# Expert lists loaded on GpSimd's queue, expert 1's rows gathered whole, and weights stored slab by slab

## The reference, cut to what matters

```python
cap = EC_FACTOR * (B * T) // N_EXPERTS          # 128 latent tokens per expert (16 of the context)
aff = jax.nn.softmax((xt @ router_w).astype(jnp.float32), axis=-1)
gate_vals, idx = lax.top_k(aff.T, cap)
xe = xt[idx]
hid = jax.nn.silu(jnp.einsum('ecd,edf->ecf', xe, w1)) * jnp.einsum('ecd,edf->ecf', xe, w3)
ye = jnp.einsum('ecf,efd->ecd', hid, w2) * gate_vals[..., None]
y = jnp.zeros_like(xt).at[idx.reshape(-1)].add(ye.reshape(-1, D))
```

## Time and profile before

| | |
|---|---|
| Median of 3 runs | 1631.14 us (1629.53 to 1637.18) |
| The profiled execution | 1631.1 us, of which the span from first to last instruction is 1629.3 us |
| PE busy | 1580.3 us (97%) |
| DVE, ACT, POOL busy | 716.6, 387.4, 477.5 us |
| DMA traffic | 324.85 MB |
| Expert part | from 849.7 us; PE then passes an expert in some 47 us |

### The profile page before, as it was taken

One profiled execution on the slowest core, in us unless ns is written; L12 is line 12 of the kernel. 1 busy time (PEld: TensorE's weight loads), 2 busy tenths in 40 slices (PEclk: granted clock), 3 DMA queues, 4 the chain that ended last, 5 costly groups with the idle time before them and its releaser, 6 DMA issues. The chain is left out here.

```text
span 1629.3 us, 28403 instructions
## 1 busy us (share of the span) xinstructions
PE 1580.3 (97%) x11180; PEld 1377.1 (85%) x11180; DVE 716.6 (44%) x1871; ACT 387.4 (24%) x970; POOL 477.5 (29%) x560
## 2 busy tenths in 40 slices
PE   6999999999999899999988999999999999999997
PEld 5866876666668767788878999999999999999997
DVE  4001046776565844222364244444334454433344
ACT  5210113341221466411131111111111111111114
POOL 3000000015232643121203343433344343334432
PEclk9999999999999999999999999999999999999999
DMA  9302212132202486423269899999899999999985
GB/s 346 114 11 85 82 39 59 36 125 30 59 29 93 133 239 204 157 66 103 91 212 353 290 299 297 316 322 298 278 293 304 291 315 329 299 286 285 315 263 228
DMA packets 225582, 324.85 MB, mean 199 GB/s; under 512 B 36015, under 2 KB 116008, under 8 KB 225466
## 3 DMA queue, kind: packets, MB, share of 16 engines
q1 hardware_dynamic: 185817, 282.70, 51.7%
q0 software_dynamic: 15568, 17.45, 5.7%
q10 hardware_dynamic: 24080, 23.02, 4.8%
HBM read 294.42 MB, written 25.51 MB: 196 GB/s over the span
## 5 line engine op out<-in xcount | busy, mean ns | idle before, releaser
L1973 PE MATMUL psum<-arena 128*128 128x144 f32 x4096 | 504.5, 286 | 1.7 <-DVE arena L2615 1.7
L1973 PEld LDWEIGHTS psum<-arena 128*128 128x128 f32 x4096 | 502.8, 190 | 1.9 <-ACT arena L1350 1.9
L1985 PE MATMUL psum<-arena 128*128 128x144 f32 x2048 | 257.3, 288 | 6.3 <-ACT arena L1391 5.0
L1985 PEld LDWEIGHTS psum<-arena 128*128 128x128 f32 x2048 | 254.8, 192 | 7.1 <-ACT arena L1391 5.2
L1556 PE MATMUL psum<-arena 128*128 128x384 f32 x720 | 242.9, 493 | 0.0
L889 POOL DMA_INDIRECT expert_list<-gt x128 | 129.8, 1014 | 317.2 <-DVE gt L2645 287.6
L1556 PEld LDWEIGHTS psum<-arena 128*128 128x128 f32 x720 | 134.5, 191 | 90.0 <-issue 2.9
L2675 DVE TENSOR_TENSOR arena<-gt,psum 128x144 f32<-128x144 f32 x128 | 38.8, 303 | 360.8 <-PE psum L1973 359.8
L2497 DVE SCALAR_TENSOR_TENSOR arena<-arena,gt 128x1024 f32<-128x1024 f32 x128 | 159.1, 1280 | 0.5 <-DMA arena<-affinity_rows 0.5
L1559 PE MATMUL psum<-arena 128*128 128x256 f32 (+2 forms) x784 | 146.4, 346 | 0.0
L1559 PEld LDWEIGHTS psum<-arena 128*128 128x128 f32 x784 | 129.4, 190 | 15.5 <-issue 1.7
(11 more groups left out here) (379 smaller groups left out, 1629.4 us busy)
## 6 DMA issues: line engine op xcount, KB each, us to landing
arena<-in_exp_w SPq DMA_DIRECT2D x96, 2048.0 KB, 11.8
arena<-in_ada_w SPq DMA_DIRECT2D x24, 1024.0 KB, 7.0
arena<-in_w_in SPq DMA_DIRECT2D x11, 1024.0 KB, 5.2
arena<-in_x_sample SPq DMA_DIRECT2D x16, 512.0 KB, 4.8
arena<-affinity_rows SPq DMA_DIRECT2D x16, 512.0 KB
arena<-m_decay_rows ACTq DMA_DIRECT2D x36, 128.0 KB, 3.2
arena<-decay_rows ACTq DMA_DIRECT2D x24, 192.0 KB, 3.4
out<-arena SPq DMA_DIRECT2D x9, 512.0 KB, 2.6
```

The lines of the kernel that those rows point to most:

```text
L1973: ins = mm(bank[:, 0:SLOTS], w[:, k, col], xeT[:, k, :], start=(k == 0), stop=(k == KD - 1))
L1985: ins = mm(bk[4 + db % 2][:, 0:SLOTS], wslot[4 + db // 4][:, k, (db % 4) * P:(db % 4) * P + P], hid[:, k, :], start=(k == 0), stop=(k == K ...
```

## The change

1. **Lists.** `load_list` leaves SP. POOL issues the list loads itself: list 1 right after it is scattered, as plain rows in one DMA; the same list again as four quarter loads inside `expert_rows(0)`; every list e + 2, in four quarter loads, right behind `expert_rows(e)`; list 15 as one DMA of rows. `expert_rows(e + 1)` begins with the wait for that list.
2. **Expert 1's rows** are gathered whole by one indirect DMA in `expert_rows(0, x_rows=True)`, and PE turns them between `hidden(0)` and `second(0)`, as it does for the last expert.
3. **Layout.** The host writes `ada_w`, `w_in`, `w_out` and the three expert matrices to DRAM slab by slab, partition by partition, so that a partition's part of a load is one run of 8 KB (slabs) or 16 KB (expert parts). SBUF holds what it held. The host's work is not in the time.

```diff
-                sp.dma_start(ring[:, s % RING, :, 0:n], w_src[mat][:, :, a:a + n]).then_inc(slab_in[s % RING], 16)
+                sp.dma_start(ring[:, s % RING, :, 0:n], slab_source(s)).then_inc(slab_in[s % RING], 16)
...
             def expert_slab(e, q):
-                one = one.rearrange("e p k f -> (e p) k f")
-                sp.dma_start(wslot[q], one[:, :, 512 * half_q:512 * half_q + 512]).then_inc(w_in_slot[q], 16)
+                src = (exp_w1, exp_w3)[q % 2][e, q // 2] if q < 4 else exp_w2[e, q - 4]
+                sp.dma_start(wslot[q], src.rearrange("p (k f) -> p k f", k=KD)).then_inc(w_in_slot[q], 16)
...
                 if e + 1 < NE:
-                    load_list(e + 1)
                     load_row(e + 2)
...
             scatter_list(1)
+            def load_list(e, rows=False):
+                pool.wait_ge(list_sc, 16 * NL * e)
+                pool.sem_inc(idx_set, 1)
+                if rows:
+                    o = 2 if e == 1 else 8 * e
+                    pool.dma_start(lists[:, o:o + 2], list_d[0:P, :]).then_inc(list_in, 16)
+                else:
+                    load_quarters(e)
+            def load_quarters(e):
+                for c in range(4):
+                    dst = lists[32 * c:32 * c + 32, bass.ds(e * 8, 8)].rearrange("p (a w) -> p a w", w=2)
+                    pool.dma_start(dst, list_d[0:P, :].rearrange("(a i) w -> i a w", i=32)).then_inc(list_in, 16)
+            load_list(1, rows=True)
...
             def expert_rows(e, x_rows=False, y_rows=False):
-                pool.wait_ge(list_in, listed(e + 1))
+                pool.wait_ge(list_in, 16 if isinstance(e, int) and e == 0 else listed(e + 1))
...
+                if isinstance(e, int) and e == 0:
+                    load_quarters(1)
+                    pool.wait_ge(list_in, listed(1))
                 scatter_list(e + 2)
...
-            expert_rows(0, y_rows=True)
-            with pool.Fori(1, NE - 2) as e:
+            expert_rows(0, x_rows=True, y_rows=True)
+            load_list(2)
+            with pool.Fori(1, NE - 3) as e:
                 expert_rows(e)
+                load_list(e + 2)
+            expert_rows(NE - 3)
+            load_list(NE - 1, rows=True)
             expert_rows(NE - 2, x_rows=True)
...
                 hidden(e)
-                if e == NE - 2:
-                    pe.wait_ge(xgl_in, fetched(NE - 1))
+                if e in (0, NE - 2):
+                    pe.wait_ge(xgl_in, fetched(e + 1))
                     pe.wait_ge(e_yeA, e + 1)
                     pe.wait_ge(e_yeD, e + 1)
                     x_turn_latent(0, KD)
...
+    def column_slabs(w, n):
+        return w.reshape(KD, P, -1, n).transpose(2, 1, 0, 3).reshape(-1, P, KD * n)
```

More of the change, by code:

```diff
@@ L66, in plan_slabs, with slab_starts @@
             + win1[4:] + win2 + [None, None] + ada[8:] + wout)
+def slab_starts(slabs):
+    starts, used = {}, 0
+    for s, slab in enumerate(slabs):
+        if slab is not None and slab[0] == "win":
+            starts[s] = used
+            used += D * slab[2]
+    return starts
 def plan_groups():
@@ L171, in hybrid_layer, with slab_source @@
     A_S = [0, 1, 3, 4, 5, 7, 8, 9]
[L172 to L175, removed]
+    in_first = slab_starts(slabs)
+    def slab_source(s):
+        mat, a, n = slabs[s]
+        if mat == "win":
+            return w_in[in_first[s]:in_first[s] + D * n].rearrange("(p k n) -> p k n", p=P, n=n)
+        return {"ada": ada_w, "wout": w_out}[mat][a // SLAB].rearrange("p (k n) -> p k n", n=n)
     def dram(name, shape):
@@ L477, in listed @@
         def listed(e):
-            return 64 * e + 1 if not isinstance(e, int) or e < NE - 1 else 64 * (NE - 2) + 17
+            return 64 * e + 16 if not isinstance(e, int) or e < NE - 1 else 64 * (NE - 2) + 32
         def fetched(e):
-            return 64 * e + 16 if not isinstance(e, int) or e < NE - 1 else 64 * (NE - 2) + 32
+            return 64 * e - 32 if not isinstance(e, int) or e < NE - 1 else 64 * (NE - 3) + 48
         def added(e):
@@ L534, in load_slab @@
                     return
-                mat, a, n = slabs[s]
+                n = slabs[s][2]
                 read = [t for t in range(s % RING, s, RING) if t in last_read]
@@ L655, in load_row @@
                                             ap=[[0, P], [1, NL * P]])).then_inc(row_in, 16)
[L657 to L665, removed]
             sp.wait_ge(r_act, 5)
@@ L674, in _ @@
                 expert_slab(0, q)
-            load_list(1)
             load_row(2)
@@ L906, in expert_rows @@
             def expert_rows(e, x_rows=False, y_rows=False):
-                pool.wait_ge(list_in, listed(e + 1))
+                pool.wait_ge(list_in, 16 if isinstance(e, int) and e == 0 else listed(e + 1))
                 pool.wait_ge(ex_full, e + 1)
-                pool.wait_ge(xgl_in, fetched(e))
+                pool.wait_ge(xgl_in, 16 if isinstance(e, int) and e == 0 else fetched(e))
                 if x_rows:
-                    pool.tensor_copy(icur[:, 0:1], lists[:, 8 * e + 8:8 * e + 9]).then_inc(idx_set, 3)
-                else:
-                    quarter_ids(icur[:, 0:4], e + 1, e * 10 + 5)
-                pool.wait_ge(idx_set, e * 10 + 5)
+                    o = 2 if e == 0 else 8 * e + 8
+                    pool.tensor_copy(icur[:, 0:1], lists[:, o:o + 1]).then_inc(idx_set, 3)
+                else:
+                    quarter_ids(icur[:, 0:4], e + 1, e * 11 + 6)
+                pool.wait_ge(idx_set, e * 11 + 6)
                 pool.sem_inc(idx_set, 1)
@@ L927, in expert_rows @@
                 else:
-                    quarter_ids(icur[:, 4:8], e, e * 10 + 11)
-                pool.wait_ge(idx_set, e * 10 + 11)
+                    quarter_ids(icur[:, 4:8], e, e * 11 + 12)
+                pool.wait_ge(idx_set, e * 11 + 12)
                 pool.wait_ge(e_yeA, e + 2)
@@ L2624, in _ @@
             dve.sem_inc(e_yeD, 1)
-            dve.sem_inc(list_in, 1)
             dve.wait_ge(acc_init, 16 * NL)
             def rank_begin(e):
-                dve.wait_ge(list_in, listed(e - 1))
+                if not isinstance(e, int) or e > 1:
+                    dve.wait_ge(list_in, listed(e - 1))
                 v.tensor_copy(acur, aff[:, 1:NT, bass.ds(e, 1)].rearrange("p a b -> p (a b)")).then_inc(rank_step, 1)
@@ L2676, in expert @@
                         .then_inc(e_hid, 1)
-                    if fb == KD - 2 and not (is_first or is_last or x_rows):
+                    if fb == KD - 2 and not (is_last or x_rows):
                         x_turned(e + 1)
-                if is_first:
-                    x_turned(e + 1)
                 if is_last:
@@ L2719, in expert @@
                 ins.then_inc(e_yeD, 1)
-            expert(0, True)
+            expert(0, True, x_rows=True)
             with dve.Fori(1, NE - 2) as e:
@@ L2759 @@
     rpb[192:-192] = rows
+    def column_slabs(w, n):
+        return w.reshape(KD, P, -1, n).transpose(2, 1, 0, 3).reshape(-1, P, KD * n)
+    w_tiles = _np.concatenate([column_slabs(w_cols[:, a:a + n], n).reshape(-1)
+                               for m, a, n in (x for x in plan_slabs() if x is not None) if m == "win"])
     order = _np.arange(D).reshape(P, KD).T.reshape(-1)
```

12 lines of the change are left out of this document (4 added, 8 removed).

## The result

The changed kernel takes 1817.75 us (median of 4 runs, 1812.44 to 1822.27) against 1632.29 us for the kernel before beside it: 1.1131 times as long, 95% interval 1.109 to 1.1173. The prediction was 1727, its range 1640 to 1790. The direction was right and the size was not; the time lies 28 us above the range. Every ratio here is of fast runs alone; one of the four runs with the layout alone (1686.17 us) was slow and is not in its ratio.

What follows compares the result with a forecast made beforehand. The prediction took PE, busy 97% of the span, as the bound, with POOL's chain only 1.4 us of slack from becoming it. 1631.1 - 1.5 - 6.0 + 103 = 1727 us, range 1640 to 1790.

Steps and rivals of the forecast that it cites:

- Start, -1.5: At the kernel's start, longer slab runs would end PE's 1.5 us wait for slabs: -1.5 us.
- Expert 1's rows, -6.0: Ahead of expert 1, rows gathered whole would nearly remove PE's 4.96 us stall: -6.0 us, bounds -3 and -7.
- `hidden(1)` at the threshold, 0: At e = 1, with only one result DMA ahead of the list loads, gathered rows would come about in time: no cost.
- Layout in the experts, 0: In the expert part PE doesn't wait for weights, so longer runs of expert weights would change nothing: 0 us.
- Lists on POOL, +103 for twelve experts: List loads join POOL's chain: 0.8 queue, 4.8 issue, 2.7 landing, 8.3 us per expert; +103 us for e = 2 to 13.
- the landing: In POOL's chain, the list loads' arrival after issue: 2.7 us, taken between SP's 1.5 and a gather's 4.4.
- X: When DVE can turn the gathered rows, T being PE's start of `hidden(e)`: median T+29.2 before, T+37.5 forecast.
- The threshold: Latest X before PE stalls in `second`: T+30.6; beyond it an expert takes (X-T)+16.6 instead of 47.04 us.
- The clock: In each of twelve experts PE runs at half speed for a while after idling: loses 1.7 us, period 55.8.
- The end: After the last `second`, DVE's last rank comes as before and nothing else moves: no cost.
- long runs hold POOL's small ones up: Rival: 16 KB weight runs delay POOL's results and gathers by 5 us more per expert: 1787, worst 1847 us; chance 0.14.
- Cheap list loads: Rival: POOL issues as quickly as SP, or lists and gathers land earlier: 1638 to 1690, likeliest about 1660 us; chance 0.15.

Runs made afterwards that it cites:

- the hold: SP issues no weight part of expert e before its gathered rows are in; on SP lists, expert 1's rows whole, whole new layout: 1622.21 us, 1644.17 without.

## Why the prediction was wrong

- **Start, -1.5**: the size fits, on more traces than these two. PE ends `hidden(0)` at 879.20 (889.77 - 10.57), before at 881.18: -2.0. One pair doesn't show it, since the end of `hidden(0)` lies between 880.5 and 884.4 in the six traces with the old slabs and between 879.2 and 883.3 in the ten with the new; their means differ by 1.5.
- **Expert 1's rows, -6.0**: wrong in sign. `hidden(1)` starts at 909.43, 905.61 before; less the start, the term is **+5.8**. The landing of the list (2.7) lay between 1.5, from a moment with the weights held back, and the gather's 4.4, from quarter rows beside runs of 2 KB. In the kernel before, SP's `load_list(1)` stood ahead of expert 1's weight parts and held them until 874.2; the change took it away, and I had costed that move at nothing ("within the bounds of the second part"). What it costs depends on the runs. From the end of `hidden(0)` to `hidden(1)` the kernel before takes 24.4 us. With rows whole and runs of 2 KB it is 23.0 (24.9 with the new slabs) with SP's list load and 22.9 with POOL's, which holds nothing back; with runs of 16 KB it is 26.1 and 30.2. So, in single traces, the move was free beside 2 KB runs and cost some 4 us beside 16 KB. In the changed kernel with the weights held, or with an eighth of them, it is 17.5: without the traffic the saving is 6.9, where 6.0 was forecast. The timeline of SP and POOL of the changed kernel:

```profile
861.59 17.97 SPq L648 DMA_DIRECT2D arena<-in_exp_w  x4
...
877.40 0.18 POOL L928 CAST gt<-gt 128x1 int32<-128x1 f32 x1 [5.10 <-DMA gt<-expert_list]
878.40 1.01 POOL L934 DMA_INDIRECT arena<-h_latent,gt  x1 [0.82 <-POOLq L932]
```

  The list lands in 5.10 us and the gather, issued by 879.41, in 10.4.
- **`hidden(1)` at the threshold, 0**: it stalled for 6.20 and cost **+8.0** (55.12 - 47.12). Lists and rows alone, with runs of 2 KB, have no stall there (47.11).
- **Layout in the experts, 0**: wrong. "Its cover is this 17 us" counted only whether the weights come in time for PE, and the loss came by way of POOL's transfers: 24 us alone, and 52 us of the twelve experts' 174 once the lists were in POOL's chain.
- **Lists on POOL, +103 for twelve experts**: the path and the form of the stall were right, and the size was **+174.0**; with runs of 2 KB it was +122. By its steps, as means of the twelve: the issue of four took 2.35, not 4.8 (direct DMAs cost POOL 0.59 each, not 0.97, so the nearest row was not near); the queue took no 0.8; **the landing is the step that failed**, 7.65 us for 2.7 (8.10 in the expert shown); and with it the gathers' landing, which the sum took over unchanged, went from 4.7 to 9.0. So X is T+43.3 for T+37.5, and the mean idle time 12.4 us for 6.8. Two errors, issue and queue, went 3.2 us the other way: had they been right, the forecast would have been lower still. The threshold was 0.2 late: 47.04 - 16.64 is T+30.4. The rule behind it, period = (X-T)+16.6, held: 41.5 + 16.6 and 2.35 of clock are 60.5, and the trace has 1025.01 - 964.55 = 60.5. The clock cost 1.8 per expert (114 instructions of `second` beyond 14.36 us, mean of the twelve), against 1.7.
- **The end**: +1.6. The terms sum to -2.0 + 5.8 + 8.0 + 174.0 + 1.6 = 187.4, the two spans differ by 1816.7 - 1629.3 = 187.4.
- **The rivals**: "long runs hold POOL's small ones up" (0.14; 1787, worst 1847) came nearest. Its 5 us per expert, 60 in all, compare with 52 measured between runs of 2 KB and of 16 KB in the twelve experts. Its mechanism, an engine that changes queues only between runs, is not shown. And it stood on a sum of 1727 that was too low beside 2 KB runs already (1755). Its counter-argument, that long runs leave the queue in 10 us, counted for nothing, since 8 us of 10 is the price. The last sign of being wrong that the prediction named, a landing of results and gathers that moves with the long runs, is what came for the gathers (6.8 with 2 KB, 9.0 with 16 KB). "Cheap list loads" was right about the issue and wrong about the sum.
- **Left open**: how a DMA engine takes turns between queues, whether the small transfers wait in the queues or for the memory behind them, and why 4 KB and 2 KB runs cost alike.

## What to carry to other kernels

Take the landing time of a small transfer only from a moment with the same traffic as the place where it is to go; here it was 1.8 us in quiet, 6 beside runs of 2 or 4 KB, 8 and more beside 16 KB. Before moving a step off a queue, ask what it held back behind it: here that was worth 4 us beside 16 KB runs and nothing beside 2 KB. Longer runs and a bulk stream with good throughput can lose on a kernel whose chain goes through small transfers, and win once the stream is kept out of their time: this layout was 0.6% slower without the hold and 0.6% faster with it.

## What the runs showed of the hardware

- Beside weight parts in flight, small DMAs issued by POOL land later than without, though the weights come from another queue: the four list loads 5.97 (4 KB runs), 6.30 (2 KB) and 8.10 us (16 KB) for 1.84, the gathers 7.7 for 1.9. At the edge it is a cliff: 3.2 us for results issued just before the parts, 7.9 for those issued 2.6 us after them.
- Four direct DMAs of POOL are issued in 2.35 us, an indirect one in 0.95 to 1.6.
- In one window at the start (22 to 24 us), slabs in runs of 8 KB move 422 GB/s where runs of 1 KB had 386:

```profile
22.00:24.00 2.00, 2.00 (x27) 1.40 (x27) 1.32 (x3) 0.55 (x1) 1.17 (x6) 1.00 1.00 422
```
- Behind a bulk stream of runs of 2 KB, four issues of SP took 7.00 us, behind runs of 16 KB 2.41. The cause was not isolated.
